# Attention step with scores and values back to back on TensorE, and a router that keeps its eight columns in the array

## The reference

```python
for layer in range(2):
    h = rms_norm(x, norm1[layer]); proj = h @ w_in[layer]
    # 8 query heads, 2 shared key/value heads, three branches
    # (compressed blocks, selected blocks, window of 512), gates; T5 bias on the logits
    o_attn = gc * o_cmp + gs * o_slc + gw * o_win       # each: softmax(q k^T * scale + bias) v
    o_conv = cb * conv3(cc * ch)                        # cb, cc, ch: 512 columns of proj each
    x = x + concat(rms_norm(o_attn), rms_norm(o_conv)) @ w_out[layer]
    h = rms_norm(x, norm2[layer])
    if layer == 0: x = x + (silu(h @ wg) * (h @ wu)) @ wd
    else:
        logits = h @ router_w + router_b                # 512 x 8
        top_logit, top_idx = top_k(logits, 2); weights = softmax(top_logit)
        x = x + weighted sum of the two chosen experts' SwiGLU (2816 wide each)
```

## Time and profile before

| | before |
|---|---|
| median of 3 runs | 2170.5 us (2169.99 to 2170.62) |
| the profiled execution | 2170.22 us, its span 2168.4 us |
| mean granted TensorE clock | 0.989 |
| busy: PE, DVE, ACT, POOL | 2127.8, 555.8, 287.2, 71.6 us |
| chain that ended last | PE 96%, DVE 2%, issue 1% |
| attention loops | about 134 to 300 us and 868 to 1034 us |
| router | about 1084 to 1118 us |
| expert weight load, issue to landing | 1536 KB, median 6.7 us |

### The profile page before, as it was taken

How to read it: one execution, slowest core, us unless ns; L and a number is a source line. 1 busy time by engine, 2 the same in 40 slices (tenths; PEclk the granted TensorE clock), 3 DMA queues, 4 the chain that set the end, 5 groups by cost and what they waited for, 6 DMA issues and landing times.

```text
span 2168.4 us, 29689 instructions
## 1 busy us (share of the span) xinstructions
PE 2127.8 (98%) x12576; PEld 1630.2 (75%) x12576; DVE 555.8 (26%) x1384; ACT 287.2 (13%) x764; POOL 71.6 (3%) x73
## 2 busy tenths in 40 slices
PE   7999999999999999999989999999999999999999
PEld 3554556888864446445489999999999998888886
DVE  2236654432334311656330010010100101010101
ACT  1123321111100112333100000000000000000000
POOL 1100000000000010000000000000000000000110
PEclk9999999999999999999989999999999999999999
DMA  8211021222240242100068567778777777888890
GB/s 325 77 39 40 1 83 49 83 112 78 92 160 0 75 189 78 40 1 1 29 260 327 220 227 262 263 271 302 264 288 265 290 280 288 313 301 303 298 348 39
DMA packets 40613, 377.38 MB, mean 174 GB/s; under 512 B 4979, under 2 KB 5011, under 8 KB 13474
## 3 DMA queue, kind: packets, MB, share of 16 engines
q1 hardware_dynamic: 34192, 355.68, 43.6%
q0 software_dynamic: 4272, 12.82, 2.3%
q10 hardware_dynamic: 2018, 7.00, 0.8%
HBM read 367.22 MB, written 10.35 MB: 174 GB/s over the span
## 4 chain that ended last, share of the span: by engine, by line
PE 96%; DVE 2%; issue 1%; ACT 0%; DMA 0%; POOL 0%; ACTq 0%; DVEq 0%; POOLq 0%
PE ps L458 31%; PE ps L1147 12%; PE ps L474 10%; PE ps L984 8%; PE ps L1163 6%; PE ps L921 6%; PE ps L468 5%; PE ps L1090 5%; PE ps L1047 2%; PE ps L1022 2%; PE ps L1035 2%; PE ps L927 1%; PE ps L898 1%; PE ps L997 1%; PE ps L415 1%
## 5 line engine op out<-in xcount | busy, mean ns | idle before, releaser
L458 PEld LDWEIGHTS ps<-work,arena 128*128 128x128 f32 x5632 | 688.4, 191 | 27.1 <-issue 26.7
L458 PE MATMUL ps<-work,arena 128*128 128x136 f32 (+3 forms) x5632 | 701.9, 283 | 0.0
L660 DVE TENSOR_TENSOR hid<-sg,ps 128x136 f32<-128x136 f32 (+3 forms) x176 | 52.7, 300 | 889.4 <-ACT sg L772 888.9
L474 PE MATMUL ps<-hid,arena 128*128 128x136 f32 (+2 forms) x1760 | 236.0, 287 | 0.0
L474 PEld LDWEIGHTS ps<-hid,arena 128*128 128x128 f32 x1760 | 225.2, 190 | 0.0
L984 PE MATMUL ps<-hT,arena 128*128 128x512 f32 x384 | 206.5, 637 | 0.0
L772 ACT ACTIVATE sg<-ps 128x136 f32<-128x136 f32 (+3 forms) x176 | 50.5, 287 | 922.1 <-PE ps L458 921.5
L1147 PE MATMUL ps<-hT,arena 128*128 128x256 f32 x704 | 155.8, 379 | 1.8 <-DVE x L1520 1.8
L1147 PEld LDWEIGHTS ps<-hT,arena 128*128 128x128 f32 x704 | 133.8, 190 | 20.5 <-issue 2.6
L921 PE MATMUL ps<-arena,hT 128*128 128x512 f32 (+1 forms) x384 | 130.3, 498 | 0.0
L468 PE MATMUL ps<-arena,hid 128*128 128x512 f32 x264 | 124.2, 593 | 0.0
(11 more groups left out here) (265 smaller groups left out, 1372.3 us busy)
## 6 DMA issues: line engine op xcount, KB each, us to landing
arena<-m_w SPq DMA_DIRECT2D x176, 1536.0 KB, 6.7
arena<-f_gu SPq DMA_DIRECT2D x11, 2048.0 KB, 7.6
arena<-w_cv SPq DMA_DIRECT2D x8, 1536.0 KB, 23.9
arena<-w_o SPq DMA_DIRECT2D x4, 2048.0 KB, 7.7
arena<-f_dn SPq DMA_DIRECT2D x4, 2048.0 KB, 7.7
arena<-w_q SPq DMA_DIRECT2D x2, 2048.0 KB, 11.2
arena<-w_kv SPq DMA_DIRECT2D x2, 2048.0 KB, 13.4
arena<-bias_by_query_and_key SPq DMA_DIRECT2D x2, 2048.0 KB, 8.8
```

The lines of the kernel that those rows point to most:

```text
L458: m = mm(ps[:, s % 2, j * CAP:j * CAP + W], w[:, k, :], xT[:, k, 0:W], start=(k == 0), stop=(k == KD - 1))
L474: m = mm(ps[:, 2 + j // 2, (j % 2) * CAP:(j % 2) * CAP + W], down_w[s % NSLOT][:, j * P:(j + 1) * P], hid[:, s % 2, 0:W], start=(s == 0 an ...
L660: v.tensor_tensor(hid[:, s % 2, 0:W], sg[:, s % 2, 0:W], ps[:, s % 2, CAP:CAP + W], ALU.mult).then_inc(hid_done, 1)
```

## The change

**Attention.** In a step, `scores(p)` and right behind it `values(p-3)` come first, with `cmp_scores` between them and `cmp_values` behind them where a step has these; then turn, fills, turn, fills. Steps from 32 on, which have no scores, stay as they were. `STEP_FILL` keeps the number of fills of every step and has none at the third place after step 2.

**Router.** The router's eight columns become the weights and the tokens move: 384 tokens at once for the first three tiles, later 128. The logits then lie with the experts on the partitions (`lgT`), are copied out of PSUM by VectorE (first part) and ScalarE (second), and turned by four small transposes. `keep_clock(n)` issues n products with 512 columns into a bank that nobody reads. On VectorE five instructions that work out the experts' order move behind the first pick.

```diff
-STEP_FILL = ((1, 1, 1), (1, 1, 1), (1, 1, 0)) + 9 * ((0, 1, 1), (1, 1, 1), (1, 1, 1))
+STEP_FILL = ((1, 1, 1), (1, 1, 1), (1, 1, 0)) + 9 * ((1, 1, 0), (2, 1, 0), (2, 1, 0))
...
                     f = STEP_FILL[p] if p < len(STEP_FILL) else (0, 0, 0)
+                    if p < NP:
+                        scores(p)
+                    if q == 4:
+                        cmp_scores(t)
+                    if 3 <= p < NP:
+                        values(p - 3)
+                    if q == 1 and 0 < t < TT:
+                        cmp_values(t - 1)
                     if 2 <= p < NP + 2:
                         turn(2 * p - 4)
-                    if p < NP:
-                        scores(p)
                     fill(f[0])
...
                     if 2 <= p < NP + 2:
                         turn(2 * p - 3)
                     fill(f[1])
-                    if p >= 3:
+                    if p >= NP:
                         values(p - 3)
-                    if q == 1 and t:
+                    if q == 1 and t == TT:
                         cmp_values(t - 1)
                     fill(f[2])
...
-                    if q == 4:
-                        cmp_scores(t)
...
         def moe_products(pe, norm_turn, turned):
 
+            def logits(bank, a, w):
+                for k in range(KD):
+                    m = mm(ps[0:E, bank, 0:w], rw[:, k, :], hT[:, k, a:a + w], start=(k == 0), stop=(k == KD - 1))
+                m.then_inc(lt_ps, 1)
+
+            def turn_logits(t):
+                return tr(ps[:, 3, E * t:E * (t + 1)], lgT[:, t * P:(t + 1) * P], ident[0:E, 0:E])
+
+            def keep_clock(n):
+                for _ in range(n):
+                    mm(ps[:, 4, :], ident, x[:, 0, 0:512], start=True, stop=True)
+
             pe.wait_ge(router_in, 32)
             turned(3, 2)
-            for t in range(TT):
-                if t == TT - 1:
-                    norm_turn(3, t)
-                    turned(3, t)
-                for k in range(KD):
-                    m = mm(ps[:, 2, E * t:E * (t + 1)], hT[:, k, t * P:(t + 1) * P], rw[:, k, :], start=(k == 0), stop=(k == KD - 1))
-            m.then_inc(rl_ps, 1)
+            logits(2, 0, 3 * P)
+            norm_turn(3, 3)
+            pe.wait_ge(lt_done, 1)
+            for t in range(3):
+                turn_logits(t)
+            turned(3, 3)
+            logits(5, 3 * P, P)
+            pe.wait_ge(lt_done, 2)
+            turn_logits(3).then_inc(rl_ps, 1)
+            keep_clock(3)
             pe.wait_ge(mask_done, 1)
...
             m.then_inc(pos_ps, 1)
+            keep_clock(2)
...
+                if L:
+                    dve.wait_ge(lt_ps, 1)
+                    v.tensor_copy(lgT[:, 0:3 * P], ps[0:E, 2, 0:3 * P]).then_inc(lt_done, 1)
                 norm_copy(2 * L + 1, TT - 1)
```

More of the change, by code:

```diff
@@ L250, in build @@
         dch = sem("dve_chain")
-        ach = sem("act_chain")
         pq_done, pkv_done, pkc_done, pcv_done = sem("pq_done"), sem("pkv_done"), sem("pkc_done"), sem("pcv_done")
@@ L338, in build @@
         pick1 = zc[:, 0:CAP]
+        lgT = qk[0:E, 1, :]
         scratch = qk[:, :, :].rearrange("p a n -> p (a n)")[:, TT * CAP:TT * CAP + 2 * E * E]
@@ L356, in build @@
         sel_ps, sel_read = sem("selected_ps"), sem("selected_read")
+        lt_ps, lt_done = sem("logits_ps"), sem("logits_copied")
         y_out, rows_in, sc_ps, out_s = sem("y_out"), [sem(f"rows_in{i}") for i in range(2)], sem("scattered_ps"), sem("out_stored")
@@ L538, in moe_vector @@
             dve.wait_ge(rl_ps, 1)
-            after(v.tensor_tensor(lg, ps[:, 2, 0:TT * E].rearrange("p (t e) -> p t e", t=TT), bc_mid(rb, 1, TT), ALU.add))
+            after(v.tensor_tensor(lg, ps[:, 3, 0:TT * E].rearrange("p (t e) -> p t e", t=TT), bc_mid(rb, 1, TT), ALU.add))
             for t in range(TT):
@@ L562, in moe_vector @@
             after(v.tensor_reduce(rank, sq1, AX, ALU.add))
[L563 to L567, removed]
             after(v.tensor_scalar(first_e, rank, 0.0, None, ALU.is_equal))
@@ L575, in moe_vector @@
                                 ALU.is_equal).then_inc(pick_done, 1)
+                if t == 0:
+                    after(v.tensor_tensor(onehot_r, bc_last(rank, E), bc_mid(i8, 1, E), ALU.is_equal))
+                    after(v.tensor_tensor(sq1, onehot_r.rearrange("p e r -> p r e"), bc_mid(i8, 1, E), ALU.mult))
+                    after(v.tensor_reduce(order, sq1, AX, ALU.add))
+                    after(v.tensor_scalar(order, order, float(FT), None, ALU.mult))
+                    v.tensor_copy(meta[:, 0:E], order[0:1, :]).then_inc(meta_done, 1)
             v.tensor_copy(mv[:, :, 0], cst[:, C_TOK:C_TOK + TT])
@@ L736, in moe_scalar @@
         def moe_scalar(se):
+            se.wait_ge(lt_ps, 2)
+            nc.scalar.copy(lgT[:, 3 * P:S], ps[0:E, 5, 0:P]).then_inc(lt_done, 1)
             se.wait_ge(max_done, 1)
```

## The result

| | before | changed |
|---|---|---|
| median (4 runs each) | 2170.53 us (2169.99 to 2170.62) | 2144.97 us (2143.16 to 2147.81) |
| the profiled execution, its span | 2170.22, 2168.4 us | 2143.16, 2141.3 us |
| mean granted clock | 0.989 | 0.994 |

The ratio is 0.9889, with a 95% interval of 0.9878 to 0.9901: faster by 25.6 us, where 22 were forecast. In a second comparison (E8) the same kernel gave 0.9904 (0.9889 to 0.9919), which is 21.7 us there; the two intervals overlap.

A forecast was written before the change was run, and what follows sets the result against it. TensorE (PE), holding 96% of the chain, was taken as the bound. Attention 14.8 us (13.8 + 2.3 + 3.3 - 4.6) and router 7.1 made 21.9 off 2170.2, giving 2148.3, said as 2148; range 2140 to 2160.

The forecast's parts named there:

- (a): Whole kernel: the gain comes as summed, within 4 us; chance 40%.
- PE's own time in the loops: Attention loops: fewer changes of array arrangement in steps 3 to 29 and around cmp_scores save 13.8 us for two layers.
- waits in steps with fills: Attention loops: 4.2 us of PE waits in both layers replace 6.5 us of waits for VectorE, gaining 2.3.
- fall of the clock at 225 and 959: Attention, both layers: the 1.2 us idle stretch goes and the half-speed clock with it, gaining 3.3 us.
- steps 30 and 31: End of each attention loop, no fills for cover: 11.5 us instead of 9.2, losing 4.6 us in all.
- router: Router: earlier logits, shorter way to the first pick and selection at full clock gain 7.1 us.
- the clock stays at half: Router: with half clock throughout, fillers included, late fillers eat the savings and the gain is about nothing.
- (d): Attention: more gain than summed, from cheaper scores-to-values or less waiting; 2139 to 2144 us, chance 5%.
- (b): Router: the clock still falls for one or more stretches; 2149 to 2152 us, at worst 2155, chance 25%.
- (c): Attention: values right behind scores are dearer, by the switch or longer copy chain; 2154 to 2157 us, chance 20%.
- (e): Attention: scores and values in direct sequence drain the array wholly; up to 35 us, time 2183, chance 6%.
- (f): Whole change gives nothing, since waits come back for all that is saved; 2166 to 2175 us, chance 4%.

The follow-up runs named there:

- E8: Changed kernel again with nothing edited, on the chip of E5 and E7: 2147.19 us, ratio 0.9904 to the kernel before.
- E5: Changed kernel with the first turn of a step moved between scores and values: 2149.01 us, ratio 0.9908 to the kernel before.
- E2: Router part of the change alone, with the attention step order and fill table of the kernel before: 2162.43 us, ratio 0.9972 to that kernel.
- E1: Attention order and fill table of the change alone, with the router of the kernel before: 2152.0 us against 2167.84, ratio 0.9927.
- E3: Changed kernel without the five filler products of keep_clock: 2147.21 us, ratio 0.9907 to the kernel before.
- E6: Changed kernel with the old logits (eight columns moving), fillers and the rest of the router kept: 2151.85 us, ratio 0.9923 to the kernel before.
- E9: Changed kernel with the five VectorE instructions for the experts' order back ahead of the first pick: 2147.11 us, ratio 0.9901 to the kernel before.
- E4: Changed kernel with steps 30 and 31 in the old order (turn, scores, turn, values): 2139.23 us, ratio 0.9871 to the kernel before.
- E7: Changed kernel with fills taken from steps 3 to 10 so that some are left for steps 30 and 31: 2138.22 us, ratio 0.9860 to the kernel before.

## Why the prediction was right, and where its terms were off

The time fell inside the range and in the likeliest case (a). By its own steps, in us:

| term | forecast | measured |
|---|---|---|
| PE's own time in the loops | -13.8 | -15.5, what the other rows leave |
| waits in steps with fills | -2.3 | -5.3 |
| fall of the clock at 225 and 959 | -3.3 | -3.2 |
| steps 30 and 31 | +4.6 | +4.4 |
| fall of the clock behind the loop | not in the sum | +1.7 in this profile |
| router | -7.1 | -6.8 |
| sum | -21.9 | -24.7, as by the marks |

The misses partly cancel: own time and waits gained 4.7 us more than was said, and a fall of the clock that the sum lacked took 1.7 of them back. That the sum came within 3 us owes something to this luck. The 25.6 us between the medians also hold the start of the program, which differs from execution to execution.

**Changes of arrangement.** The prices worked out from the earlier trace rows held: a step with three fills lasts 5.69 where 5.67 was said, and is 0.25 shorter than before where 0.27 was said. The sum's weakest value, nothing extra for values directly behind scores, held too: 1.06 from start to start. But it isn't a change without a price: scores before work of their own kind take 0.96. What the step saved is one change of four. Such a change is worth more than the 0.10 in front of it that the prediction names, 0.25 by the step and 0.19 by E5, since the work behind it pays as well; the step sums had that in, the sentence had not. By the Trainium skill (TensorEngine Tiling (Array Packing), Key Properties) every change of the tiling mode drains TensorE. The trace agrees, with 0.10 ahead of the change, between scores and values too. What the term missed is `cmp_scores`, here before the change (start 269.09, 1.01 to the turn behind it):

```profile
268.03 1.13 PE L984 MATMUL ps<-hT,arena 128*128 128x512 f32 x2
269.09 1.08 PE L1059 MATMUL ps<-kcT,arena 64*128 64x31 f32 x16
270.10 0.66 PE L1035 MATMUL ps<-cst,arena 128*128 128x128 f32 x4
```

It cost 1.17 with its neighbours (0.10 on the fill ahead, 1.01, 0.06 on the turn behind); between scores and values it costs 0.81 (0.91, less 0.10 that the scores in front save). That is 0.36, not 0.15, in three of the four tiles and 0.24 in the first: about 1.4 us more over eight.

**Waits.** This is the term that was mis-sized. Its step was a loop of 5.2 us against a short step of 4.81 that would make values wait 0.4 at four tiles and 0.2 at three. Behind the short steps values did not wait at all. PE waited elsewhere in the short step, ahead of its second turn, which needs VectorE's copy of the first: some 0.2 at four tiles and 0.1 at three. Listed waits came to 1.6 us in both layers where 4.2 were said. So the sign that the prediction named, idle time ahead of values in place of that ahead of the turns, is seen only in step 31 (0.37). The loop itself was right: where nothing covers it, from turn to turn at 263.90 and 269.08, it takes 5.18. But it is not run in every step. VectorE and ScalarE start a step's copies by when PE's turn is done, and the long steps on both sides give back what the short one lacks; the estimate took each short step as if it stood in a row of short ones. Only one wait of some length was left in layer 0 outside the last steps, 0.72 at step 19. That the long steps' slack is what absorbs it was argued from these rows and not tried by itself.

**The clock in the loop.** None of the nine profiles with the new step (E5's variant among them) shows a fall in the steps with fills, in either layer. So the term stands, against this profile of before; its size is E2's 1.6 (150.15 less 148.57), twice. E2 also shows that the fall isn't certain even in the old step.

**The end of the loop.** 11.42 us to the first turn of step 32 where 11.5 was said, and T to T 5.18. Two things follow that the sum hadn't: the wait of 2.00 us is longer than any that this loop had, and in layer 1 the clock is at half right behind it (998.4, above), 1.7 us more on the output products. E1, E3, E6 and E9 show the same fall in both layers, E8 in layer 1 alone; E4, E5 and E7, whose longest wait there is 1.29, 1.89 and 0.67 us, in neither. E7 is the plain remedy, since fills in steps 30 and 31 are worth more than in steps 3 to 10, where the short copies of one or two tiles need little cover.

**The router.** Logits 5.26 (5.15 said), mask 12.5 behind the output products (12.3), selection 9.66 (9.5), its end 25.8 (25.5). The three parts can be taken apart now. The orientation of the logits decides: with the old one and everything else as changed (E6) the router is at its old length, 33.90. The fillers are worth 2.1 (E3) and the order on VectorE 1.1 (E9). These three don't add up to the whole, since behind narrow logits the fillers cost time. That E6 equals the router of before (33.90 and 33.86) is a coincidence, and no test of the prediction's case "the clock stays at half": its mask product comes 4.1 later, and the positions and the selection take 4.1 less. The new logits with neither fillers nor the new order on VectorE were not run.

**The rivals.** (a) and (d): by the median the time lies 1 us above the range of (d), whose condition, less waiting, came true. (b): the clock was at full through the router in all seven profiles that had the new logits and fillers, the tiny turns and two waits included. The Trainium skill (TensorE: Matmul & The Clock Gate, Part 4: PE-mode transpose) says that transposes don't count as busy for the clock; by that page it could have fallen here, and the trace doesn't show it, with 1.0 us of transposes between two products. At the start of the program the trace says more: PE's first work is 16 transposes from 12.18 on, and the clock rose at 15.4, when it had run nothing else (they go 0.21 apart, then 0.11). So these did count. (c): refuted by 1.06 from scores to values and by waits of 1.6 us. (e): refuted by the same 1.06. (f): the waits came back only in two steps of 32.

## What to carry to other kernels

Price a new order of work on TensorE by start-to-start times of neighbours, kind by kind. Group the work that uses a part of the array, and count what each change of arrangement costs, ahead of it and behind it (a step with one change less was 0.25 us shorter here, most of some 15 us over two layers). Keep independent work back for the last steps of a loop: two steps without it cost more here than all the others together. Where a product is narrow on the moving side, make the narrow operand the weights; here that kept the clock up through the logits, which fillers behind the narrow products could not do.

## What the runs showed of the hardware

**The moment at which the clock first rises shifts the whole program.** In the changed kernel's profile it rises at 15.4, two transposes before the end of the first 16, and the next eight take 1.09 us; in E5's, the transposes at 18.22 still go at half, and the clock rises at 23.8. The scores of step 2 come 2.0 us later there.

```profile
12.18 3.61 PE L917 MATMUL ps<-cst,work 128*128 128x128 f32 x16 [12.18 <-DVE work L1312]
...
17.12 1.09 PE L917 MATMUL ps<-cst,work 128*128 128x128 f32 x8 [0.17 <-DVE work L1312]
```
```profile
18.22 3.67 PE L917 MATMUL ps<-cst,work 128*128 128x128 f32 x16
```

Over the eleven profiles the rise lies between 15.0 and 24.0 us; in E7 it is at 16.5, with another fall from 19.9 to 23.3. A fall of the clock near 97 us, in a stretch with 64 records of 24 moving columns and no idle time, is in each of them and lasts 6.8, 10.2 or 13.7 us; the same stretch in layer 1 has one between 818 and 833 in each. The rise and the first of these falls go with where the scores of step 2 stand, 131.05 (E3) to 135.72 (before). That is up to 4.7 us of the end time from one execution to the next, more than the 0.2% that the medians can tell, and 2.4 of the 27.0 us between the two profiles. Stretches inside the program repeat to some 0.01 us where the clock is the same, so for effects of 1 or 2 us they, not the medians, are the measure.

**The same idle time doesn't always bring the clock down.** The 1.24 us of E2 did in layer 1 and didn't in layer 0; the 2.00 us at the end of the changed loop did in layer 1 and not in layer 0, and in E3 in both. Each fall cost about 1.6 us. What decides it these runs don't show.
